# Filler products on TensorE between an attention and the first expert of a decoder trunk

## The reference

```python
def moe(xn, w_router, w_gate, w_up, w_down):
    logits = (xn @ w_router).astype(jnp.float32)
    top_val, top_idx = lax.top_k(logits, TOP_K)
    top_w = jax.nn.softmax(top_val, axis=-1)
    gates = jnp.sum(jax.nn.one_hot(top_idx, N_EXPERTS, dtype=jnp.float32) * top_w[..., None], axis=-2)
    ...
        hg = jnp.einsum('sd,edf->sef', xs, w_gate)
        hu = jnp.einsum('sd,edf->sef', xs, w_up)
        hh = jax.nn.silu(hg) * hu * gs[..., None].astype(xs.dtype)
        return jnp.einsum('sef,efd->sd', hh, w_down)
```

## Time and profile before

| what | value |
|---|---|
| runs | 1302.27, 1305.60, 1305.85 us, median 1305.6 |
| profiled execution | 1306.33 us, its span 1304.5 us |
| TensorE busy | 1236.1 us, 95% of the span |
| mean granted clock of TensorE | 0.986 |
| dense part and attentions | up to about 436 us |
| experts | from 452.94 us to the end |

### The profile page before, as it was taken

The page is one execution under the profiler, slowest core; times in us unless marked ns, Lnnn a source line. Parts: engine busy times, 40 slices in busy tenths (PEclk is TensorE's granted clock), DMA queues, the critical chain, the costliest instruction groups (busy, mean ns, idle before and its releaser), DMA issues.

```text
span 1304.5 us, 20307 instructions
## 1 busy us (share of the span) xinstructions
PE 1236.1 (95%) x8367; PEld 631.0 (48%) x8368; DVE 321.9 (25%) x728; ACT 252.0 (19%) x446; POOL 27.9 (2%) x44
## 2 busy tenths in 40 slices
PE   6999999999899899899999998899999999999997
PEld 4765777778665633333433433333343343334333
DVE  2363576667253510000001010011001001000102
ACT  2251433333154111001101101101100110211111
POOL 2100000000100010000000000000000000000000
PEclk9999899999999799999999999999999999999999
DMA  9511645326612479999989999999999999999993
GB/s 340 202 65 58 238 156 194 129 100 243 247 72 99 186 315 427 419 419 417 408 302 408 427 418 420 428 419 418 426 420 397 425 423 420 422 422 408 382 427 139
DMA packets 73168, 413.71 MB, mean 317 GB/s; under 512 B 6606, under 2 KB 11852, under 8 KB 64636
## 3 DMA queue, kind: packets, MB, share of 16 engines
q1 hardware_dynamic: 71708, 409.59, 77.9%
q0 software_dynamic: 1088, 1.81, 0.4%
q10 hardware_dynamic: 288, 1.05, 0.2%
HBM read 411.38 MB, written 1.05 MB: 316 GB/s over the span
## 4 chain that ended last, share of the span: by engine, by line
PE 84%; DMA 5%; DVE 4%; issue 3%; ACT 2%; SPq 2%; POOL 0%; DVEq 0%; ACTq 0%; POOLq 0%
PE ps L1392 16%; PE ps L1372 10%; PE ps L1459 7%; PE ps L1367 6%; PE ps L1350 6%; PE ps L1093 4%; PE ps L1089 4%; PE ps L1090 4%; PE ps L1354 3%; PE ps L1423 3%; PE ps L1443 3%; PE ps L1341 2%; DMA ring<-in_moe_w_up 2%; PE ps L1074 2%; DMA ring<-in_moe_w_down 2%
## 5 line engine op out<-in xcount | busy, mean ns | idle before, releaser
L1392 PE MATMUL ps<-ring,arena 128*64 128x448 f32 x640 | 255.0, 550 | 18.9 <-issue 10.2
L1393 PE MATMUL ps<-ring,arena 128*64 128x448 f32 x640 | 255.3, 551 | 0.0
L1392 PEld LDWEIGHTS ps<-ring,arena 128*64 128x64 f32 x640 | 84.9, 138 | 168.0 <-issue 155.5
L1372 PE MATMUL ps<-ring,arena 128*32 128x448 f32 x1152 | 162.1, 541 | 0.0
L1373 PE MATMUL ps<-ring,arena 128*32 128x448 f32 x384 | 160.8, 541 | 0.0
L1940 DVE TENSOR_TENSOR arena<-arena,ps 64x448 f32<-64x448 f32 (+1 forms) x64 | 38.5, 614 | 376.5 <-ACT arena L879 197.7
L1459 PE MATMUL ps<-ring,arena 128*64 128x512 f32 x280 | 124.7, 595 | 3.2 <-DMA ring<-in_moe_w_down 3.2
L1460 PE MATMUL ps<-ring,arena 128*64 128x512 f32 x280 | 124.7, 595 | 0.0
L1367 PE MATMUL ps<-ring,arena 128*32 128x448 f32 x768 | 91.1, 546 | 8.4 <-DVE arena L1940 4.0
L1372 PEld LDWEIGHTS ps<-ring,arena 128*32 128x32 f32 x1152 | 47.9, 111 | 95.3 <-issue 95.3
L1675 DVE TENSOR_TENSOR w_lo<-ring,w_hi 128x2048 fp32r<-128x2048 f32 x33 | 75.5, 2292 | 63.3 <-ACT w_hi L777 61.8
(11 more groups left out here) (301 smaller groups left out, 1460.2 us busy)
## 6 DMA issues: line engine op xcount, KB each, us to landing
ring<-in_moe_w_down SPq DMA_DIRECT2D x64, 1792.0 KB, 18.2
ring<-in_moe_w_gate SPq DMA_DIRECT2D x127, 896.0 KB, 15.2
ring<-in_moe_w_up SPq DMA_DIRECT2D x127, 896.0 KB, 16.6
ring<-in_ffn_w_gate SPq DMA_DIRECT2D x5, 2048.0 KB, 7.8
ring<-in_ffn_w_up SPq DMA_DIRECT2D x5, 2048.0 KB, 7.8
ring<-in_ffn_w_down SPq DMA_DIRECT2D x5, 2048.0 KB, 7.7
ring<-in_mla_w_o SPq DMA_DIRECT2D x2, 2048.0 KB, 24.4
ring<-in_swa_w_q SPq DMA_DIRECT2D x2, 2048.0 KB, 8.3
```

Of the source, the lines that this page charges most:

```text
L1372: pe.matmul(ps[32 * j:32 * j + 32, c, 0:CH], thirds[j], wu[:, c * CH:(c + 1) * CH], start=first, stop=last)
L1392: pe.matmul(ps[0:NARROW, c, 0:CH], lhs, wu[:, cols], start=(k == 0), stop=(k == KD - 1))
L1393: mm = pe.matmul(ps[64:64 + NARROW, c, 0:CH], lhs, wg[:, cols], start=(k == 0), stop=(k == KD - 1))
```

## The change

A function `keep_busy(bank, n)` multiplies the identity matrix by the first `n` columns of the constants and writes the result to a PSUM bank whose content is no longer needed. Nobody reads it. It waits for nothing and signals nothing. It is called at three places: once with 256 columns between `router(1, 0)` and `h_to_T(1, 1)`, twice with 512 columns between `router(1, 1)` and the wait for `route_mask`, and twice with 512 columns between `gather()` and the wait for `counts_ready`.

```diff
@@ -1312,6 +1312,10 @@
                 if half == 1:
                     mm.then_inc(s.router_mm, 1)
 
+            def keep_busy(bank, n):
+
+                pe.matmul(ps[:, bank, 0:n], ident, cst[:, 0:n], start=True, stop=True)
+
             swo_product(2, range(KD), True, True)
             h_to_T(0, 0)
             h_to_T(0, 1)
@@ -1321,8 +1325,11 @@
             router(0, 0)
             router(0, 1)
             router(1, 0)
+            keep_busy(5, 256)
             h_to_T(1, 1)
             router(1, 1)
+            keep_busy(7, 512)
+            keep_busy(7, 512)
 
 
             pe.wait_ge(s.route_mask, 1)
```

## The result

The changed kernel took 1295.07 us (median of 4 runs, 1294.12 to 1298.57) against 1305.72 for the kernel before (4 runs). The ratio is 0.9928, with a 95% interval of 0.9903 to 0.9954. The forecast was 1306.8, in a range of 1302.9 to 1310.0: it was wrong, by about 12 us and in its sign. The profiled execution took 1298.57 us, its span 1295.9.

The account below looks back on a forecast made before the run. The prediction took TensorE (busy 95% of the span) as the bound, every microsecond before the first expert counting at the end. Terms of +1.18 us on the profiled 1306.33 gave 1307.5, or 1306.8 on the median; range 1302.9 to 1310.0.

Parts of the forecast that it names:

- the change part by part: Step pricing each filler and the first expert's first products where they stand, summed to +1.18 us.
- The local sum: Router to first expert: 0.43 + 1.77 + 0 + 0.91 - 1.93 = +1.18 us.
- First filler: Between router(1,0) and h_to_T(1,1): no wait hides it, clock falls as before, +0.43 us (bounds -0.60 and +0.43).
- Second filler: After router(1,1): at half clock it delays the count products by 1.77 us; other bound 0.06.
- Third filler: Behind the gather: +0.05 us at full clock, +1.77 at half; the middle, +0.91, taken.
- First steps: First expert's five first steps: gap closed, so full clock, 1.87 us instead of 3.80, -1.93 us.
- low-clock rival: Clock stays low through to the first expert, gather slow too: +5.4 us, 1311.0 us; chance 0.15.
- the clock holds: First filler keeps the clock full through router(1,1) and onward: -2.66 us, 1302.9 us; chance 0.2.
- It doesn't arrive: Experts' weights set the end and the ring absorbs a shift of a few microseconds: 1305.6 us; chance 0.1.
- three signs of being wrong: Clock 1.00 from 439 to 453; expert's first steps still 0.75 us; transfers restarting before the first expert ran ten microseconds.
- The rival by which only long gaps cost the clock: No filler can hold the clock, so fillers only cost: +3.97 us, 1309.6 us; chance 0.1.

Follow-up runs that it names:

- padding alone: Kernel before, no fillers, with 20 semaphore increments nobody waits for at the head of TensorE's list: 1294.96 us, ratio 0.9933; again on another chip 1293.23 us, ratio 0.9928.
- the third filler alone: Kernel before with only the two 512-column products behind the gather, plus 12 idle semaphore increments at the head of TensorE's list: 1291.24 us, ratio 0.9914.
- half the third filler: Kernel before with only one 512-column product behind the gather, plus 4 idle semaphore increments at the head of TensorE's list: 1293.59 us, ratio 0.9913.

## Why the prediction was wrong

The step that failed is "the change part by part". It lists what each filler costs where it stands, and sums that. What was left out is that added instructions move all code behind them. The prediction took the kernel outside the stretch as unchanged, a term of nothing without a reason. In the traces items 3, 6 and 8 became 5.1, 4.65 and 3.4 us shorter, 13.2 together, and padding alone gives the same ratio. The row was there to be read: four "issue" waits of 10.2 us at L1392 among the waits of the kernel before, of which the prediction explains only the one of 1.67 us before the first expert. I didn't ask what the other three were, though they stand just behind a branch. That the code's place decides is shown by the experiments. By which rule a place is good, with 4, 8, 20 and 60 instructions and not with 0, 128 and 256, stays open.

The local sum itself held:

- First filler: +0.43 forecast. Router(1,1) starts 4.34 us after the first router record instead of 3.85, +0.49, and the clock fell all the same (1.88 us for the eight records).
- Second filler: +1.77 forecast, 2.45 - 0.49 = +1.96 measured, at half clock.
- Third filler: +0.91 forecast, 3.12 - 2.45 = +0.67 measured.
- First steps: -1.93 forecast, -1.78 measured. That one is right for this execution; the padding alone shows that it isn't always there to be had.

Together +1.34 against +1.18. On one chip and with the loop's place held, the whole of the fillers costs 4.0 us by the medians, nearer to the low-clock rival (+5.4) than to the sum. The clock over the gather was indeed 0.50 in the changed kernel, for some 6.1 of its 6.7 us, but back at the third filler. The two traces lie 2.5 us apart (spans of 1293.3 and 1290.8): the later start of 3.25 us with no gain at the first steps behind it, 0.9 more in the stage, and 1.6 less ahead of the router.

Of the rivals, "the clock holds" didn't happen; the sign of the result agrees with it and its cause doesn't. "It doesn't arrive" was partly right: in item 4 a lead of 1.68 us shrank to 0.35, since the weights set the pace there. The transfers did restart two microseconds later (SyncE's first issue at 464.95 instead of 462.98), as the argument from the earlier trace rows said. Of the prediction's three signs of being wrong only the last was seen: they restarted 464.95 - 456.69 = 8.26 us after the first expert's start, not ten. But that follows from the gain that the sum itself counts on: 10.04 us before, less the 1.78 by which the first steps became faster. So the sign was badly chosen, and none of the three looked outside the stretch. The rival by which only long gaps cost the clock played no part: the clock fell again after the gap of 0.8 us, and behind the third inner gap of the kernel before, 2.85 us long, it didn't.

The chances gave 0.08 to "faster by more than 0.3%". With the moved code among the rivals, at three gaps of 2.8 us that could go and one placement in several that is bad, that would have been a case of ten microseconds with a chance worth naming.

## What to carry to other kernels

When a change adds or removes instructions in front of a loop with large bodies and branches, look first at the "issue" waits at the branch targets and just behind them, before and after, and at the count of instruction fetches. To test whether a gain is the change's own, add the same number of idle instructions in its place; and to test whether a loop lies badly, add a few in front of it. Here four were enough for 0.6%, and the version to keep is the padding, or the third filler alone, without the first two.

## What the hardware showed that I had not expected

- Four idle instructions before a loop whose two bodies show 876 and 2572 product and load records (a narrow expert from 762.9 to 862.0 us, a wide one from 545.5 to 670.4) took away three waits of 2.8 us, and with them the slow clock behind two of them: 0.6% of the time. Padding of 8 and 60 gave 0.8%, with overlapping intervals.
- The narrow expert that follows a narrow one fetches nothing: between 755 and 865 us the DMA view of the kernel before shows no instruction fetch at all, though the 876 records of its body are more than three blocks of 256 (and 256 instructions more in front of the loop made one fetch more). So TensorE holds several blocks. The page of the Trainium skill named above gives both a larger store for TensorE and, a little further on in the same section, two blocks for all; the run is against the latter.
- A semaphore increment at the head of TensorE's list costs about 0.15 us. With 60, 108 and 128 of them TensorE's first product came at 10.1, 17.4 and 20.5 us, where it comes at 9.6 without: (20.5 - 10.1) / 68 = 0.153 us for each further one, and 0.155 over the last 20.
- The length of a gap alone doesn't tell whether the clock falls. It fell behind gaps of 0.8 us (after thin router products) and 1.67 us, and stayed at 1.00 behind one of 2.85 us between full-clock steps (1202.38 us, kernel before) and one of 1.58 us (half the third filler).
